# Two transformer blocks on one core: convolution steps and the compressed attention's weights reordered, and six products of the second block moved from GpSimd to VectorE

## The reference, cut to what matters

```python
h = rms_norm(x, norm_mix_pre[l])
proj = h @ w_in[l]
...
k_cmp, v_cmp = nsa_compress(...), nsa_compress(...)      # 15 compressed keys and values per group
o_cmp, p_cmp = nsa_compressed_attention(qa, k_cmp, v_cmp)
o_slc, o_win = ...                                       # attention over all keys, twice
o_a = ga[:, :, 0] * o_cmp + ga[:, :, 1] * o_slc + ga[:, :, 2] * o_win
o_b = conformer_conv(b_in, conv_w[l], conv_b[l], conv_ln_g[l], conv_ln_b[l])
o_c = pool_mixer(c_in, pool_w[l], pool_scale[l])
o_d = banded_attention(...)                              # with sinks
up = jnp.einsum("bsnc,ncd->bsnd", jnp.stack([o_a, o_b, o_c, o_d], 2), w_branch[l])
gates = jax.nn.sigmoid((h @ w_gate[l]).reshape(bsz, seq, 4, 1024))
x = x + rms_norm(jnp.einsum("bsnd,bsnd->bsd", gates, up) @ w_o[l], norm_mix_post[l])
...                                                      # then the feed-forward part
```

```
h_t = exp(dt_t A) h_{t-1} + dt_t B_t x_t ;  y_t = C_t . h_t     # in both directions, in chunks of 128 tokens
y = y_f + y_b + xs * d_skip
```

## Time and profile before

| | us |
|---|---|
| median of three runs | 1821.84 (1820.89 to 1829.63) |
| the profiled execution | 1830.08 |
| its span, first to last instruction | 1828.0 |
| PE busy | 1680.5 |
| DVE busy | 1084.7 |
| ACT busy | 760.2 |
| POOL busy | 261.6 |

### The profile page before, as it was taken

How to read it: one execution, slowest core, us unless ns; L and a number is a source line. 1 busy time by engine, 2 the same in 40 slices (tenths; PEclk the granted TensorE clock), 3 DMA queues, 4 the chain that set the end, 5 groups by cost and what they waited for, 6 DMA issues and landing times. The chain is left out here.

```text
span 1828.0 us, 26603 instructions
## 1 busy us (share of the span) xinstructions
PE 1680.5 (92%) x10712; PEld 1383.9 (76%) x10712; DVE 1084.7 (59%) x1490; ACT 760.2 (42%) x1069; POOL 261.6 (14%) x293
## 2 busy tenths in 40 slices
PE   7998997899998989998899989999898978999996
PEld 5887897699977888887799974445475537899995
DVE  4668987566645668987566631284547334454555
ACT  4355654455534355554455422113116224333431
POOL 0200004144301200003144200014320000000000
PEclk9999998899999999998899999999869987999998
DMA  6544454466553545454466554112000232355551
GB/s 252 185 185 162 185 185 151 149 234 250 184 200 139 211 157 184 169 178 158 151 237 224 187 185 170 69 69 91 25 23 1 70 115 93 139 184 184 184 182 70
DMA packets 40121, 282.07 MB, mean 154 GB/s; under 512 B 4816, under 2 KB 5072, under 8 KB 6864
## 3 DMA queue, kind: packets, MB, share of 16 engines
q1 hardware_dynamic: 38432, 273.15, 41.4%
q10 hardware_dynamic: 1584, 7.42, 1.2%
HBM read 279.50 MB, written 1.05 MB: 153 GB/s over the span
## 5 line engine op out<-in xcount | busy, mean ns | idle before, releaser
L428 DVE TENSOR_TENSOR ring_low<-ring,sb_hi 128x2048 fp32r<-128x2048 f32 x116 | 267.9, 2309 | 192.3 <-ACT sb_hi L423 191.9
L423 ACT ACTIVATE sb_hi<-ring 128x2048 fp32r<-128x2048 f32 x116 | 222.5, 1918 | 285.9 <-DMA ring<-weights 114.4
L577 PE MATMUL psum<-sb_hS,sb_hi 128*128 128x256 f32 x704 | 203.3, 289 | 4.8 <-DVE ring_low L428 4.7
L1848 DVE TENSOR_TENSOR sb_split<-ring,sb_split 128x2048 fp32r<-128x2048 f32 x48 | 109.9, 2292 | 153.2 <-ACT sb_split L1843 153.2
L580 PE MATMUL psum<-sb_hS,sb_hi 128*128 128x256 f32 x704 | 200.3, 284 | 0.0
L581 PE MATMUL psum<-sb_hS,ring_low 128*128 128x256 f32 x704 | 199.4, 283 | 0.0
L839 PE MATMUL psum<-sb_hfT,ring_low 128*128 128x256 f32 x704 | 198.1, 281 | 0.0
L2162 PE MATMUL psum<-sb_hfS,sb_split 128*128 128x256 f32 x512 | 146.5, 286 | 6.0 <-DVE sb_hfS L2692 3.9
L2165 PE MATMUL psum<-sb_hfS,sb_split 128*128 128x256 f32 x512 | 145.8, 285 | 0.0
L2166 PE MATMUL psum<-sb_hfS,sb_split 128*128 128x256 f32 x512 | 145.8, 285 | 0.0
L577 PEld LDWEIGHTS psum<-sb_hS,sb_hi 128*128 128x128 f32 x704 | 134.9, 192 | 14.1 <-DVE ring_low L428 7.2
(11 more groups left out here) (392 smaller groups left out, 3881.7 us busy)
## 6 DMA issues: line engine op xcount, KB each, us to landing
ring<-weights SPq DMA_DIRECT2D x256, 1024.0 KB, 4.8
sb_rows_ffn<-rows ACTq DMA_DIRECT2D x4, 512.0 KB, 4.7
sb_rows_mix<-rows ACTq DMA_DIRECT2D x2, 1024.0 KB, 5.0
sb_rows<-rows ACTq DMA_DIRECT2D x1, 2048.0 KB, 9.1
sb_x<-x_in SPq DMA_DIRECT2D x2, 512.0 KB, 5.9
sb_y<-ctx_in SPq DMA_DIRECT2D x1, 1024.0 KB, 6.4
out<-sb_x SPq DMA_DIRECT2D x2, 512.0 KB, 2.7
sb_const<-const SPq DMA_DIRECT2D x1, 711.0 KB, 13.5
```

Of the source, the lines that this page charges most:

```text
L423: act.activation(hi_of(n), ring[:, c % SLOTS, :], ACT.Copy).then_inc(hi_ready, 1)
L428: eng.tensor_tensor(low_of(n), ring[:, SPLIT_CHUNKS[n] % SLOTS, :], hi_of(n).bitcast(F32), ALU.subtract).then_inc(lo_dve, 1)
L577: mm = pe.matmul(out, hi[:, k, bs], hS[:, 0, k, :], start=(k == 0), stop=False)
L1848: dve.tensor_tensor(split[:, n % SPLITS, 1, :], ring[:, (first_moe + n) % SLOTS, :], split[:, n % SPLITS, 0, :].bitcast(F32), ALU.subtract ...
```

## The change

- In round 1, `cmp_weigh` comes ahead of the low part of the gate chunk on DVE.
- The rounds hold 4, 18, 16, 10, 10, 12 and 20 steps of the convolution (90) in place of 12 each (84). Behind each product of the branches come 4 steps, ahead of the low part, in place of 3 or 5 behind it.
- The convolution's transposes come before job (0, 2) in place of (0, 3), the transposes back before (3, 0) and (3, 1) in place of (3, 1) and (3, 2), and DVE's low parts of the convolution's branch after (3, 1), before the low part of a chunk, in place of after (3, 2). POOL takes the inverse roots ahead of all its additions. ACT splits chunk `FIRST_UP + 6` after both tiles' SiLU, not between them.
- In the second block, the six products `xdt` and `y` move from POOL to DVE, behind `dw`; POOL begins with `wx`.

```diff
-CONV_BEFORE = (0, 3)
-OB_BEFORE = {(3, 1): 0, (3, 2): 1}
+CONV_BEFORE = (0, 2)
+OB_BEFORE = {(3, 0): 0, (3, 1): 1}
+CONV_STEPS = (4, 18, 16, 10, 10, 12, 20)
...
         for t in range(TT):
-            if t == 1:
-                split_hi(act, FIRST_UP + 6)
             jobs.wait_filled(act, ("obT", t))
...
-        for n in range(FIRST_UP + 7, FIRST_WO + 1):
+        for n in range(FIRST_UP + 6, FIRST_WO + 1):
             split_hi(act, n)
...
+            if r == 1:
+                cmp_weigh()
             split_lo(dve, FIRST_GATE + 2 * r + 1)
             if r == 0:
                 pool_low()
                 cmp_blocks()
-            if r == 1:
-                cmp_weigh()
...
-            conv_steps(12)
+            conv_steps(CONV_STEPS[r])
...
                 if (n, i + 1) == CONV_BEFORE:
                     conv_norm()
-                if (n, i + 1) == (3, 3):
-                    for t in range(TT):
-                        dve.wait_ge(ob_hi, t + 1)
-                        part = brS[1][:, :, :, t * P:(t + 1) * P]
-                        dve.tensor_tensor(part[:, 1, :, :], acc[:, :, t * P:(t + 1) * P], part[:, 0, :, :].bitcast(F32),
-                                          ALU.subtract).then_inc(ob_lo, 1)
-                if i % 2 == 0:
-                    conv_steps(3)
-                else:
+                conv_steps(4)
+                if i % 2 == 1:
                     chunk = 2 * bi + i // 2
+                    if chunk == 4:
+                        for t in range(TT):
+                            dve.wait_ge(ob_hi, t + 1)
+                            part = brS[1][:, :, :, t * P:(t + 1) * P]
+                            dve.tensor_tensor(part[:, 1, :, :], acc[:, :, t * P:(t + 1) * P], part[:, 0, :, :].bitcast(F32),
+                                              ALU.subtract).then_inc(ob_lo, 1)
                     if chunk < 7:
                         split_lo(dve, FIRST_UP + chunk + 2)
-                    conv_steps(5 if chunk < 2 else 4 * TAPS)
...
+        conv_roots()
         k = 0
         for n in BRANCH_ORDER[1:]:
...
-                if (n, i + 1) == CONV_BEFORE:
-                    conv_roots()
...
             dve.tensor_tensor(dw[:, :, :], dw[:, :, :], dt[:, :, :], ALU.mult).then_inc(dw_ready, 1)
+            for i in range(SEQ_TILES):
+                for half in range(2):
+                    jobs.wait_filled(dve, ("xsT", i, half))
+            for t in range(TT):
+                for half in range(2):
+                    jobs.wait_drained(dve, ("xsT", 2 + t, half))
+                x3 = xs[:, 2 + t, :].rearrange("p (h c) -> p h c", c=DH)
+                for d in range(2):
+                    dve.tensor_tensor(xdt[:, 2 * t + d, :].rearrange("p (h c) -> p h c", c=DH), x3,
+                                      bc(dt[:, 2 + t, 16 * d:16 * d + 16].unsqueeze(2), [P, 16, DH]), ALU.mult).then_inc(xdt_ready, 1)
+                dve.tensor_tensor(y[:, t, :].rearrange("p (h c) -> p h c", c=DH), x3, bc(R("skip").unsqueeze(2), [P, 16, DH]),
+                                  ALU.mult).then_inc(skip_ready, 1)
...
             pool.wait_ge(dt_ready, 1)
-            ... (the same waits and six products, on pool)
             pool.wait_ge(dw_ready, 1)
```

More of the change, by code:

```diff
@@ L2837, in _ @@
             pool.wait_ge(dt_ready, 1)
[L2838 to L2849, removed]
             pool.wait_ge(dw_ready, 1)
```

## The result

The changed kernel takes 1806.91 us (median of six, 1803.54 to 1809.56), the kernel before 1825.74 (median of six on the same chips, 1818.73 to 1830.31). The ratio given with the runs is 0.9892, 95% interval 0.9867 to 0.9918: 19.7 us faster (15.0 to 24.3). The forecast was 1798 us and 23.6 us of gain. The changed kernel's profiled execution took 1803.91 us with a span of 1801.8, so the two profiled spans lie 26.2 us apart.

What follows compares the result with a forecast made beforehand. PE was taken to bound the kernel, busy 1680.5 of 1828.0 us, with two waits on DVE to shorten. 4.5 + 8.8 - 1.5 = 11.8 us a layer, 23.6 in all, gave 1821.84 - 23.6 = 1798 us, range 1791 to 1809.

Steps and rivals of the forecast that it cites:

- Part 1: Rounds: moving cmp_weigh ahead and taking 8 steps from round 0 gains 4.5 us a layer, bounds 1.6 to 6.9.
- the wait 6.0 to 0.7: Round 1: PE's wait for the compressed attention's weights shrinks from 6.0 to 0.7 us, 5.3 us gained.
- new waits 1.1 and 2.2: Rounds: PE newly waits for low parts, 1.1 us behind the compressed weights and 2.2 us in round 2.
- half of that time is lost: Half-clock stretches behind the two longest waits, 5.4 and 4.6 us, lose 2.7 and 2.3 us.
- Part 2: Branches: reordering around the convolution's last step gains 8.8 us a layer, less 1.5 us for the clock behind the new wait.
- The wait 8.2 to 2.8: Branches: PE's wait ahead of the convolution's transposes shrinks from 8.2 to 2.8 us, 5.4 us gained.
- The wait ahead of (1, 0): Branches: PE's 1.3 us wait before job (1, 0) goes, since ACT and DVE finish the next chunk before PE arrives.
- The loss behind the new wait: Convolution's transposes: half clock behind the 2.8 us wait costs 1.5 us a layer, bounds 0 and 2.9.
- Part 3: Second block: moving six products from POOL to DVE gains 0, bounds -0.5 to 0.5 us, since nothing arrives earlier.
- The clock takes more: Rival: two new waits a layer each bring half clock costing 2.9 us; 7.5 us a layer gained, 1807 us; chance 0.14.
- DVE gives the first gain back: Rival: 18 and 16 steps in rounds 1 and 2 keep making low parts late; 7.3 a layer, 1807 us; chance 0.11.
- Slower: Rival: the convolution's last step ends late; 13.3 us late eats the gains, 18 us late gives 1831 us; chance 0.03.

Runs made afterwards that it cites:

- fourteen_later: Changed kernel with 14 more steps before the branches, 7 each in DVE's idle time of rounds 4 and 6; 0.9853 of the kernel before.
- roots_behind: Changed kernel with POOL's inverse roots back behind its additions up to (0, 1); 0.9923 of the kernel before.
- five_in_round1: Changed kernel with 5 of round 1's 18 steps put ahead of its second low part, where DVE stands idle; 0.9862 of the kernel before.
- changed_again: The changed kernel once more, nothing altered; 1806.26 us against 1830.13 for the kernel before, 0.9885.
- part1_rounds: Kernel before with only cmp_weigh ahead of the low part and rounds of 4, 18, 16, 10, 10, 12, 14 steps; 1822.81 us against 1828.18, 0.9982.
- twelve_steps_late: Changed kernel with 8 steps in round 6 in place of 20, and 7 behind each branch product in place of 4; 0.9949 of the kernel before.
- steps_in_gaps: Changed kernel with 19 convolution steps put in DVE's idle gaps, 5 in round 1, 7 in round 4, 7 in the last; 1795.38 us, 0.9836.
- Part 3 alone: Kernel before with only the six products moved to DVE and POOL beginning with wx; 1829.04 us against 1828.18, 1.0006.
- gaps_no_first_steps: The kernel with 19 steps in DVE's gaps, with no step in round 0 where it had 4; 1795.40 us, 0.9818 of the kernel before.

## Why the prediction was right, and what was off

**Part 1, mechanism right, one term missing.** Forecast 4.5 us a layer; measured 4.6 in layer 0 and 3.5 in layer 1 of the changed kernel. Its steps: the wait 6.0 to 0.7, gain 5.3 (measured 0.66, gain 5.37); new waits 1.1 and 2.2 (0.89 and 1.96); last 18 steps 7.1 us (7.21); PE's lead at the scores of round 2 6.9 us (148.15 against 156.78, with the rounds begun 2.0 earlier: 6.6). The opening names the stretches at half clock in the order of time and not of the waits: 5.4 us stand behind the compressed weights and 4.6 behind the convolution, and the sums use them so. The term "half of that time is lost", 2.7 and 2.3 us, was a little too high: counted to the same matmul at full clock, PE lost 2.4 and 2.1. The step that failed is "bounds 1.6 to 6.9, I take 4.5": I let no half clock follow the 2.2 us wait. By the stage clocks of the table's kernels, it followed in 12 of the 14 layers that had this wait (all but layer 0 of the changed kernel and of fourteen_later, the two that took 139.0 and 138.9 us). It costs 1.1 to 1.4 us (3.4 us at half) where the rounds take 140.1 to 140.4, and 2.5 to 2.7 (6.8 at half) where they take 141.5 to 141.7. Over the four layers of the two profiled executions the rounds average 140.3 us against 143.75 before: 3.4 us a layer, not 4.5. The lower bound, 1.6, had the right mechanism; its 2.9 us loss was too much.

**Part 2, right.** Forecast 8.8 - 1.5 = 7.3 us a layer; measured 7.4 and 7.5. The wait 8.2 to 2.8, gain 5.4: measured 2.86, gain 5.38. The wait ahead of (1, 0): gone. A step beside POOL: none above 0.42 us, and roots_behind shows what it was worth. The loss behind the new wait, put at 1.5 us between 0 and 2.9: 3.4 us at half clock in 7 of the 10 layers that have this wait, none in 3. PE is busy for 37.54 us of the stage with it (the window above) and for 36.2 without (36.22 in layer 0 of five_in_round1), 1.3 us, of which 0.3 come back in a shorter wait behind. So 1.0 us, not 1.5; with the 2.1 given back for 2.3, the two errors nearly cancel. Half clock followed in all six layers that also have the wait of round 2, and in one of the four that don't; what decides isn't shown. The Trainium skill ("TensorE: Matmul & The Clock Gate", section "Why this matters for your kernels") advises against idle gaps between bursts of matmuls, from a length on that lies a little above this wait. The traces agree with it in direction: a fall behind 7 of 10 waits of 2.8 to 2.9 us, and behind 12 of 14 of about 2, shorter than the page names.

**Part 3, right: 0.** 715.6 us with and without it, ratio 1.0006 (0.9986 to 1.0027). POOL's first `wx` was forecast near 1257 less the gain: 1233.95 us, with PE 23.2 us earlier at the start of the second block.

**The sum.** Rounds and branches gave 23.0 us in the first profiled pair and 20.5 in the second (against the same execution of before), where 23.6 was forecast; the timed executions give 19.7 (15.0 to 24.3) and, for changed_again, 0.0115 x 1830.1 = 21.0. What the pairs miss, 0.6 and 3.1 us, lies in the rounds (8.1 and 5.6 us where 9.0 were forecast), where half clock followed the wait in round 2 in one layer of the first execution and in both of the second. In absolute time the miss is 8.7 us (1798.2 for 1806.9). By the medians 3.9 of it are the base, since I subtracted from a median of three executions, 1821.84, and six gave 1825.74; the other 4.8 are the gain, 18.8 us between these medians for 23.6. Beside changed_again the base read 1830.13 and the medians lay 23.9 us apart, so there nearly the whole miss is the base. The kernel before was timed between 1817.8 and 1831.0 us in all.

**The rivals.** "The clock takes more" (1807) named the cause of the shortfall and gave its time almost exactly, but through 2.9 us behind both waits; measured are about 1.3 and 1.0. Its gain, 15.0 us, stands at the edge of the interval (15.0 to 24.3); that 1807 is the measured time owes 3.9 us to the base, which is luck. "DVE gives the first gain back" fell with part1_rounds: the convolution's wait stayed at 8.2 us, and no later low part was late. "Slower" needs 13.3 us of lateness; twelve_steps_late measured its price, 5.6 us for 4.9 us of steps. At that price, an estimate from this one run, the 10.8 us that a layer gained (3.4 and 7.4) would be eaten at 9.5 us of lateness, not at 13.3.

**The 3.0 us in the second block.** These stretches of before:

```profile
1330.70:1358.00 27.30, 27.30 (x105) 22.86 (x105) 12.13 (x32) 5.11 (x9) 9.36 (x8) 0.50 0.00 1
```

and of the changed kernel, at the corresponding place:

```profile
1308.20:1318.40 10.20, 10.20 (x35) 7.44 (x34) 5.08 (x13) 1.89 (x3) 4.45 (x4) 0.50 0.01 4
1318.50:1325.20 6.70, 6.70 (x57) 6.19 (x56) 5.45 (x16) 2.20 (x4) 2.53 (x2) 1.00 0.00 1
1325.30:1332.10 6.80, 6.80 (x21) 4.26 (x20) 3.12 (x7) 1.30 (x3) 2.49 (x2) 0.50 0.00 0
```

PE is busy throughout in both; one has full clock in the middle and the other hasn't. The table tells which executions: 712.5 or 712.6 us in three (both of the changed kernel, one of steps_in_gaps), 715.6 to 716.7 in the other eleven, of which six have part 3. Part 3 alone doesn't bring it (715.6), and without part 3 the time is the same (0.9893). What decides in which form an execution runs there stays open; both profiles of the changed kernel had the shorter one, where I had expected the longer in most.

## What to carry to other kernels

When a profile shows a wait on an engine that itself stands idle somewhere earlier, fill that idle time before you reorder anything: 19 steps moved into three gaps of DVE gave 13 us in the traces and some 10 in the timed ratios, on top of the reordering, and they took away the two waits, of 2.0 and 2.9 us, that it had left. Price a wait with what follows it: a wait of 2 to 3 us was followed by half clock in 19 of 24 layers, and that added 1.0 to 2.7 us to it. And forecast a difference, then apply it to many timed executions; a median of three lay 4 to 8 us below the later ones here, more than any term of the sum was off.

## What the runs showed of the hardware that I had not expected

- A wait of about 2 us (1.9 to 2.1) between stretches in which PE is fully busy was followed by half clock, for 3.4 or 6.8 us, in 12 of 14 layers, and the same wait of the same kernel in another execution by none (rounds of 139.0 and 141.5 us). A wait of 1.3 or 1.4 us, in gaps_no_first_steps, was followed by full clock in both layers (granted 1.00).
- At half clock matmuls of this kernel start 0.21 us apart and not 0.12, so that 3.4 us at half lose 1.6. Where a later wait absorbs a part, the stage loses less: 1.0 us.
- PE can show no idle time for 27.3 us and be granted half its clock for all of it (105 matmuls in the second block of the kernel before). The profile models the ends of matmuls, so this says that PE had work, not that it was at its peak.
- A step of the convolution on DVE takes 0.40 to 0.42 us alone; four steps, with an addition on POOL beside 1.4 of their 2.7 us, took 0.67 each (roots_behind).
